# Forgetting attention in a two-block network: head sums moved later, scores negated, rounds written out, and the shared zone at a multiple of 128 bytes

## What is computed

```python
k = rmsnorm(k_s, k_norm)                      # per head, over 64 features
c = cumsum(log_sigmoid(f_logit))              # one number per head and token
q = rmsnorm(qg[..., :d], q_norm)
s = einsum('qd,kd->qk', q_i, k) * 64 ** -0.5 + c_i[..., None] - c[None, :]
s = where(kpos <= qpos, s, -inf)              # causal, blocks of 128 queries
p = softmax(s, axis=-1)
o = einsum('qk,kd->qd', p, v) * sigmoid(qg[..., d:])
x = x + o @ b_w_out
```

## Time and profile before

| | |
|---|---|
| median of three runs (lowest to highest) | 2271.34 us (2270.18 to 2273.8) |
| the profiled execution | 2267.01 us |
| its span, first to last instruction | 2265.3 us |
| share of the span busy: PE, POOL, DVE, ACT | 96%, 52%, 47%, 38% |
| mean granted TensorE clock | 0.989 of 2.4 GHz |
| the rounds, from the end of the first K unit to the output layer | about 1544 to 1855 us |

### The profile page before, as it was taken

How to read it: one execution, slowest core, us unless ns; L and a number is a source line. 1 busy time by engine, 2 the same in 40 slices (tenths; PEclk the granted TensorE clock), 3 DMA queues, 4 the chain that set the end, 5 groups by cost and what they waited for, 6 DMA issues and landing times.

```text
span 2265.3 us, 31096 instructions
## 1 busy us (share of the span) xinstructions
PE 2174.4 (96%) x9968; PEld 1744.3 (77%) x9968; DVE 1059.3 (47%) x1870; ACT 871.6 (38%) x1270; POOL 1175.9 (52%) x1572
## 2 busy tenths in 40 slices
PE   6999999799999999999999999998999989999999
PEld 5777666588888888888788888886677768888887
DVE  5466677533345543123435555115667664545400
ACT  6344223433344433232244443234444444443421
POOL 7443322777655555645456556654333325655653
PEclk9999999899999999999999999999999999999999
DMA  6213411233322233323223322332222202232332
GB/s 221 80 47 107 121 48 32 69 94 93 113 92 98 97 101 95 93 93 102 93 84 102 102 93 88 102 102 79 76 75 65 82 30 93 93 102 95 95 101 71
DMA packets 61469, 204.92 MB, mean 90 GB/s; under 512 B 6848, under 2 KB 6976, under 8 KB 61392
## 3 DMA queue, kind: packets, MB, share of 16 engines
q1 hardware_dynamic: 61200, 203.65, 28.1%
q10 hardware_dynamic: 192, 0.30, 0.1%
HBM read 201.52 MB, written 2.39 MB: 90 GB/s over the span
## 4 chain that ended last, share of the span: by engine, by line
PE 81%; DVE 8%; DVEq 4%; ACT 3%; issue 2%; POOL 1%; DMA 1%; ACTq 0%; SPq 0%
PE bank L1305 26%; PE bank L1307 26%; PE bank L1306 25%; PE bank L1513 1%; DVEq L1225 1%; DVE FX L1216 1%; PE bank L1567 1%; PE bank L1346 1%; DVE FX L1207 0%; DVE SS L1227 0%; DVEq L1231 0%; POOL YL L469 0%; DMA RAW<-in_w_att 0%; POOL WL L413 0%; ACT TD L729 0%
## 5 line engine op out<-in xcount | busy, mean ns | idle before, releaser
L413 POOL TENSOR_TENSOR WL<-RAW,WH 128x256 fp32r<-128x256 f32 x1496 | 1147.2, 800 | 1057.1 <-ACT WH L501 1056.9
L1305 PE MATMUL bank<-XH,WH 128*128 128x512 f32 x1840 | 730.2, 397 | 2.8 <-DVE XQ L821 2.0
L1307 PE MATMUL bank<-XH,WL 128*128 128x512 f32 x1840 | 716.7, 390 | 0.0
L1306 PE MATMUL bank<-XL,WH 128*128 128x512 f32 x1840 | 716.3, 389 | 0.0
L501 ACT ACTIVATE WH<-RAW 128x1024 fp32r<-128x1024 f32 x374 | 392.1, 1051 | 225.8 <-PE bank L1307 213.6
L1305 PEld LDWEIGHTS bank<-XH,WH 128*128 128x128 f32 x1840 | 345.4, 188 | 81.8 <-issue 6.6
L1306 PEld LDWEIGHTS bank<-XL,WH 128*128 128x128 f32 x1840 | 345.5, 188 | 76.3 <-issue 5.0
L1307 PEld LDWEIGHTS bank<-XH,WL 128*128 128x128 f32 x1840 | 345.4, 188 | 72.7
L1305 PE MATMUL bank<-FH,WH 128*128 128x512 f32 x528 | 208.0, 394 | 0.0
L1307 PE MATMUL bank<-FH,WL 128*128 128x512 f32 x528 | 207.0, 392 | 0.0
L1306 PE MATMUL bank<-FL,WH 128*128 128x512 f32 x528 | 204.9, 388 | 0.0
(11 more groups left out here) (276 smaller groups left out, 2342.1 us busy)
## 6 DMA issues: line engine op xcount, KB each, us to landing
RAW<-in_w_up SPq DMA_DIRECT2D x132, 512.0 KB, 3.5
RAW<-in_w_att SPq DMA_DIRECT2D x47, 512.0 KB, 3.6
RAW<-in_w_down SPq DMA_DIRECT2D x48, 448.0 KB, 3.3
RAW<-in_w_fa SPq DMA_DIRECT2D x32, 512.0 KB, 3.5
RAW<-in_w_down SPq DMA_DIRECT2D x24, 512.0 KB, 3.5
RAW<-in_w_ain SPq DMA_DIRECT2D x24, 512.0 KB, 3.5
RAW<-in_w_mrg SPq DMA_DIRECT2D x18, 512.0 KB, 3.6
RAW<-in_w_mrg SPq DMA_DIRECT2D x22, 256.0 KB, 2.7
```

The source lines that it names most:

```text
L413: last = nc.gpsimd.tensor_tensor(WL[:, s, w], RAW[:, s, w], WH[:, s, w].bitcast(F32), ALU.subtract)
L1305: mm(dst[:, 0:width], WH[:, s, w], a, start=start and k == 0, stop=False)
L1306: mm(dst[:, 0:width], WH[:, s, w], b, start=False, stop=False)
L1307: last = mm(dst[:, 0:width], WL[:, s, w], a, start=False, stop=stop and k == kc - 1)
```

## The change

1. **The zone** starts at the next multiple of 128 bytes. `HOLD` is gone; the fixed part ends at 135584 and the zone starts at 135680, which is 1060 times 128.
2. **Later head sums.** PE does the unit first and the head sum after it (K's sum after Q's unit, Q's after V's, V's transposes after the gate's unit). The raw head goes straight into `FK` or `FQ`. DVE uses it one group later than before, with four instructions for each head instead of six, and ACT reads the sum from PSUM itself.
3. **Negated scores.** The Q gain, the mask and the decay carry the opposite sign, the custom instruction finds a minimum, and that is the bias ACT needs: `HOLD` and the negation (L1211) go.
4. **The gate's** three ACT instructions move to the start of the next round, behind the exponentials of group 0.
5. **Rounds written out**, on all engines, instead of the loop.

```diff
-    zone = top[0]
+    zone = (top[0] + 127) // 128 * 128
...
-        with engine.Fori(0, (FA_PAIRS - 2) // 2) as i:
-            round_(2, i)
-            round_(3, i)
...
+        for p in range(FA_PAIRS + 1):
+            round_(p)
...
+        def squared(p, s):
+            act.wait_ge(q_raw, 2 * p + s + 1)
+            if 2 * p + s:
+                act.wait_ge(q_sum, 2 * p + s)
+            A_(SQ[:], (FK, FQ)[s][:, p % 2, :], ACT.Square).then_inc(q_sq, 1)
+        def head_rstd(p, s):
+            act.wait_ge(q_sum, 2 * p + s + 1)
+            if 2 * p + s:
+                act.wait_ge(f_epi, 2 * p + s)
+            A_(TD[:], LB[(O["fa"] + FA_L * p + 2 + 2 * s) % 2][:], ACT.Ln, scale=1.0 / 64, bias=EPSC[:, 0:1])
+            act.drain()
+            A_(TD[:], TD[:], ACT.Exp, scale=-0.5).then_inc(q_rs, 1)
...
+        def round_(p):
             for s in range(4):
                 if p < FA_PAIRS:
+                    hi(U["fa"], 4 * p + s + AHEAD, 0, 0)
+                if p < FA_PAIRS and s >= 2:
+                    head_rstd(p, s - 2)
                 if p >= 1:
...
+                        act.wait_ge(fs_read, 2 * g + j + 1)
+                        A_(FX[:, j, 0:nk], FX[:, j, 0:nk], ACT.Exp, scale=-1.0, bias=NX[:, j:j + 1],
                            accum_out=RS[:, j:j + 1]).then_inc(fp_exp, 1)
+                    if s == 0:
+                        out_gate(p - 1)
                 if p < FA_PAIRS and s < 2:
+                    squared(p, s)
...
+        def raw_head(p, s):
+            dve.wait_ge(unit_done, U["fa"] + 4 * p + s + 1)
+            v.tensor_tensor((FK, FQ)[s][:, p % 2, :], LB[(O["fa"] + FA_L * p + s) % 2][:], R[:], ALU.mult)\
+                .then_inc(lin_free, 1)
+            dve.drain().then_inc(q_raw, 1)
+        def head_sums(p, s):
+            dve.wait_ge(q_rs, 2 * p + s + 1)
+            v.scalar_tensor_tensor(out=SS[:], in0=LB[(O["fa"] + FA_L * p + 2 + 2 * s) % 2][:],
+                                   scalar=64 * EPS, in1=TD[:], op0=ALU.add, op1=ALU.mult).then_inc(lin_free, 1)
+            head = (FK, FQ)[s][:, p % 2, :]
+            v.scalar_tensor_tensor(out=head, in0=head, scalar=col(("kn", "qn")[s]), in1=TD[:],
+                                   op0=ALU.mult, op1=ALU.mult)
+            dve.drain()
+            v.scalar_tensor_tensor(out=SS[:], in0=SS[:], scalar=-0.5 / 64, in1=TD[:], op0=ALU.mult, op1=ALU.mult)
+            dve.drain()
+        def head_done(p, s):
+            head = (FK, FQ)[s][:, p % 2, :]
+            v.scalar_tensor_tensor(out=head, in0=SS[:], scalar=1.5, in1=head, op0=ALU.add, op1=ALU.mult)\
+                .then_inc(f_epi, 1)
...
-                        v.tensor_tensor(HOLD[:], EPSC[:, 0:1], EPSC[:, 1:2], ALU.add)
...
+                                               scale=1.0, scalar=-NEG, op0=ALU.add, op1=ALU.min,
+                                               accum_out=NX[:, j:j + 1]).then_inc(fs_read, 1)
+                if p < FA_PAIRS and s >= 2:
+                    head_sums(p, s - 2)
...
+                    f_unit(p, s, o0 + (0, 1, 3, 5)[s])
+                    if s == 1:
+                        f_sums(p, 0, o0 + 2)
+                    if s == 2:
+                        f_sums(p, 1, o0 + 4)
                     if s == 3:
+                        f_turn(p, o0 + 6)
```

More of the change, by code:

```diff
@@ L437, in _ @@
             pool.drain()
-            nc.gpsimd.affine_select(out=NM[r], in_=NM[r], compare_op=ALU.is_ge, fill=NEG, base=0,
+            nc.gpsimd.affine_select(out=NM[r], in_=NM[r], compare_op=ALU.is_ge, fill=-NEG, base=0,
                                     pattern=[[-64, 2], [1, P]], channel_multiplier=-1)
@@ L712, in o_split, with out_gate, round_ @@
             A_(AH[:, n, :], FY[:, n, :], ACT.Copy).then_inc(oh_ready, 1)
-        def round_(p, i=0):
+        def squared(p, s):
[10 more added lines that the diff above has]
+            A_(TD[:], TD[:], ACT.Exp, scale=-0.5).then_inc(q_rs, 1)
+        def out_gate(p):
+            g = FG[:, p % 2, :]
+            act.wait_ge(f_g, p + 1)
+            A_(g, g, ACT.Exp, scale=-1.0)
+            act.drain()
+            A_(g, g, ACT.Ln, bias=ONES[:, 0:1])
+            act.drain()
+            A_(g, g, ACT.Exp, scale=-1.0).then_inc(fg_ready, 1)
+        def round_(p):
             for s in range(4):
                 if p < FA_PAIRS:
-                    hi(U["fa"], 4 * p + s + AHEAD, i, 8)
+                    hi(U["fa"], 4 * p + s + AHEAD, 0, 0)
+                if p < FA_PAIRS and s >= 2:
+                    head_rstd(p, s - 2)
                 if p >= 1:
@@ L748, in round_ @@
                     act.dma_start(fc_d[:, :], FC[:, 1, :]).then_inc(fc_out, 16)
[L749 to L755, removed]
                 if p >= 1:
                     for j in range(2):
-                        act.wait_ge(ft_full, i * 16 + (2 * g + j + 1))
+                        act.wait_ge(ft_full, 2 * g + j + 1)
                         if g >= 1:
-                            act.wait_ge(fpv, i * 16 + (2 * g + j - 1))
+                            act.wait_ge(fpv, 2 * g + j - 1)
                         A_(FP[:, j, 0:nk], TRB[j][:, 0:nk], ACT.Copy).then_inc(ft_out, 1)
@@ L1218, in round_ @@
                 if p < FA_PAIRS:
[L1219 to L1245, removed]
                     if s >= 2:
-                        dve.wait_ge(unit_done, i * 8 + (U["fa"] + 4 * p + s + 1))
-                    b = LB[(o0 + (0, 2, 4, 6)[s]) % 2]
+                        head_done(p, s - 2)
                     if s < 2:
+                        raw_head(p, s)
                         if p == 0 and s == 0:
@@ L1515, in f_products, with f_unit, f_sums, f_turn @@
                 last.then_inc(fpv, 1)
-        def round_(p, i=0):
+        def f_unit(p, s, o):
+            pe.wait_ge(lin_free, o + 1)
+            xh, xl = ((XH, XL), (AH, AL), (XH, XL), (AH, AL))[s]
+            unit(U["fa"], 4 * p + s, 0, 0, KB, xh, xl, 0, LB[o % 2],
+                 ready=(al_ready, KB) if p == 0 and s == 1 else None)
+        def f_sums(p, s, o):
+            pe.wait_ge(lin_free, o + 1)
+            pe.wait_ge(q_sq, 2 * p + s + 1)
+            mm(LB[o % 2][:], BLK[:], SQ[:], start=True, stop=True).then_inc(q_sum, 1)
+        def f_turn(p, o):
+            pe.wait_ge(lin_free, o + 1)
+            pe.wait_ge(f_src, p + 1)
+            for k in range(TB):
+                last = nc.tensor.transpose(LB[o % 2][:, P * k:P * (k + 1)], TC[:, P * k:P * (k + 1)], IDN[:])
+            last.then_inc(f_trs, 1)
+        def round_(p):
             o0 = O["fa"] + FA_L * p
```

128 lines of the change are left out of this document (47 added, 81 removed).

## The result

The changed kernel takes 2259.18 us, median of five runs (2255.58 to 2261.66), against 2271.34, which is a median of five runs too, and not of three as the table of before has it; the ratio is 0.9948, 95% interval 0.9937 to 0.9960. It is faster by 0.5%, 12.2 us, where 27.8 were forecast; the time lies above the forecast range. The profiled execution took 2260.75 us with a span of 2259.0.

The account below looks back on a forecast made before the run. PE, busy 2174.4 of 2265.3 us, was taken as the bound, so gains come from its idle time, half clock or pace. 6.9 + 6.3 + 12.7 + 1.9 = 27.8 us off 2271.3 gives 2243.5 us; range 2236 to 2254.

Parts of the forecast that it names:

- Part 1: Matmul steps on zone tiles: starting the zone on a 128-byte line gains 6.9 us, bounds 0 and 7.5.
- the loop's 1 us: Rounds written out instead of looped: upper bound of the gain, 1 us, from branches; the forecast itself was 0.
- Part 2: Round 0, first K unit to first scores: Q's unit following at once shortens PE's stalls by 6.3 us, bounds 4.5 and 8.
- Part 3: Rounds 1 to 7: PE's waits before head sums and V's transposes vanish, 12.7 us, bounds 5 and 13.
- Part 4: Last round, without units: a shorter chain from scores to normalisation gains 1.9 us, bounds 0 and 4.
- Part 5: Rounds written out instead of the loop: gain 0, within 1 us either way.
- The zone's address means nothing: Rival on the zone's tiles: only the order counts, gain 20.9 us, time 2250.4 us; chance 0.16.
- Slack eaten: Rival for the seven rounds: a later ACT chain makes PE wait, 7 to 8 us lost, 2251 us; shared chance 0.16.
- slower: Rival: a much longer chain makes PE wait twice a round, slower than before, 2286 us with 3 us each; chance 0.04.
- Round 0 and the tail keep their stalls: Rival: first and last rounds keep their waits and half clock, 2251 us; shared chance 0.16.

Follow-up runs that it names:

- b_zone_up64: Kernel before the change with only the zone's start moved 64 bytes up, to the changed kernel's address; 2283.4 us, ratio 1.0058 to before.
- a_zone_64: Changed kernel with its zone 64 bytes lower, at the old address, leaving the new order; 2250.2 us, ratio 0.9911 to the kernel before.
- a_zone_plus128: Changed kernel with its zone 128 bytes further up, at 135808, the weights' remainder modulo 256; 2243.71 us, ratio 0.9882 to the kernel before.
- a64_chain_back: Changed kernel, zone at the old address, with tiny DVE instructions like HOLD and the negation put back around each custom instruction; 2251.66 us, ratio 0.9914 to before.

## Why the prediction was wrong, step by step

**Part 1 failed, and it accounts for the miss.** The step was "If a start off a 128-byte line costs the 7 ns". The rows had shown rightly that the pace with `FH` and `AH` differs from that with `XH` and that distance and stage do not explain it. What I took for the cause, a start off a 128-byte line, was one guess about a difference that has other properties: `XH` and the weights have the same remainder modulo 256, and the zone did not. Moving it from 64 to 128 bytes away made it worse. Measured in place of a gain of 6.9 us: a loss of 13 us (`b_zone_up64`), which 880 steps by 13.3 ns put at 11.7 (12.6 with `GH`'s 64). With this exchanged the forecast would have been 2243.5 + 6.9 + 11.7 = 2262; the time was 2259.2. The bound of this part was 0 on the bad side, and that closed the range too early. (The range's other end was added up wrongly: the upper bounds of parts 1, 2 and 4 and the loop's 1 us give 2243.5 - 0.6 - 1.7 - 2.1 - 1 = 2238.1, not 2236.) A step at 0.700, `GH`'s, stood in the earlier trace rows with the same start as `FH`: it said that a slower level exists, though the later profiles don't show it at that address. I read it as an extra gain to be had, not as the level to which the others could fall.

Of the Trainium skill, "TensorE: Matmul & The Clock Gate", part 1, gives one distance between warm matmuls, N/2.4 GHz plus about 2.5 ns. It names no address; that the distance holds wherever the operands lie was my reading. The runs differ, with 0.680 to 0.704 us for three matmuls by address alone, and the measurement decides. That the zone at a multiple of 128 would gain nothing, which I had worked out from that page and from the 16-byte cachelines that the Trainium skill gives in "SBUF — State Buffer", Specifications, was nearer to the result than my forecast.

**Part 2, round 0** was forecast at 6.3 us. From the norm to the first scores, before 1578.36 - 1537.9 = 40.5 us. The changed kernel on this stretch:

```profile
1559.95 0.51 PE L1308 MATMUL bank<-AH,WH 128*128 128x512 f32 x1 [1.97 <-DVE AL L1177]
...
1572.19 1.12 PE L1531 MATMUL bank<-SQ,BLK 128*128 128x512 f32 x2 [0.83 <-DVE SS L1204]
...
1575.81 0.79 PE L1308 MATMUL bank<-AH,WH 128*128 128x512 f32 x1 [2.50 <-DVE TC L1259]
...
1584.48 0.50 PE L1556 MATMUL bank<-FK,FQ 64*128 64x128 f32 x4
```

After it is 1584.48 - 1548.1 = 36.4, a gain of 4.1. In `a_zone_64` the scores start at 1570.91, 33.6 us after the norm, a gain of 6.9, and in `a_zone_plus128` 35.2 us after it, 5.3. The waits stand where they were worked out: the second half of `AL`, Q's sum behind the bank (0.83 us, forecast 1.1), the gate's unit behind the read of V (2.50, forecast 2.0). What varies is the half clock. Its stretches in this window sum to 10.2 us in the changed kernel (36.4 us) and in `a64_chain_back` (36.5), to 6.8 in `a_zone_plus128` (35.2) and to 3.4 in `a_zone_64` (33.6). The wait of 2.50 us is in all of them; in the changed kernel the clock falls to half at 1574.4, inside that wait, and stays there for 6.8 us. I had counted the half clock once and for another place. The gains of 4.1, 5.3 and 6.9 us lie around the 6.3 forecast and follow the half clock.

**Part 3, rounds 1 to 7**, 12.7 us: the mechanism and its size were right. The same three windows in the kernel before:

```profile
1537.90:1578.36 40.46, 29.62 (x108) 0.87 0.09 29
1578.36:1833.61 255.25, 242.57 (x1358) 1.00 0.24 80
1833.61:1906.10 72.49, 65.80 (x325) 0.93 0.18 59
```

From the first scores to those of the last round, 255.25 us became 243.36 in `a_zone_64`, 11.9 less. In the changed kernel the round fell by 1.7 us to 34.92, of which 16 steps with `AH` at 13 ns more take 0.2. No wait took the place of the old ones, but for 1.0 us for the normalised rows at the start of round 1 in `a_zone_64`, and `a64_chain_back` shows the slack. I was wrong on a side point: that `HOLD` and the negation gain nothing on PE is true of rounds 1 to 7 in the new order only.

**Part 4, the last round**, 1.9 us, was too small, within its bounds: 72.5 us became 69.4 in `a_zone_64`, 3.1 less, and 69.1 in `a_zone_plus128`, whose granted clock there is the 0.93 of before and of whose gain the 64 faster steps make 0.4. I had put `HOLD` at 0.15 us, where the earlier trace rows has a mean of 0.318. **Part 5**, 0, was right as far as can be measured. Parts 2 to 5 together: forecast 20.9, measured 20.3 by the median and 21.9 between the norms of `a_zone_64`, in the one of its four executions with a granted clock of 0.992 (the others had 0.988). No run moves the gate's three instructions (part 4 of the change) by themselves, so their share is not known.

**The rivals.** "The zone's address means nothing" had 0.16 and was wrong in the same direction: no case of mine had an address that costs. "Slack eaten" and "slower" are refuted by the waits. "Round 0 and the tail keep their stalls" is refuted too: both became shorter, by 6.9 and 3.1 us in `a_zone_64`.

## What to carry to other kernels

Where the rows show that one tile is faster than another, they don't show which of its properties makes it so. Before moving anything, list all that the fast one shares with its partners (here the remainder of the weights it is multiplied with), and give each reading its own sign and price. If matmuls run back to back, it is worth trying moving operands and weights at one remainder modulo 256: here it was worth 6.6 us alone, and 15 us against a round-looking address.

An instruction on DVE is free or not by the order around it: the same pairs cost PE 0.7 us a round where the next head waited behind them, and nothing in the steady rounds where the head was due one group later.

## What the runs showed of the hardware that I had not expected

- Three back-to-back matmuls of 512 columns take 0.680 us when the starts of the moving operands and of the weights agree modulo 256 bytes (up to 0.686 straight behind matmuls for which they don't). With both moving tiles 64, 128 and 192 bytes off they take 0.687, 0.697 and 0.700 with TensorE alone; in the whole kernel 64 bytes off gave 0.687 and 128 bytes off 0.700, and 192 was not run. Between two kernels that differ in nothing else, 64 bytes made 13 us of 2270.
- Starts that are no multiple of 64 behave irregularly (0.694 at +16, 0.680 at +240). Moving one operand of the four costs 6 to 24 ns in no order that I can state. No run shows the cause. Why `GH` had 0.700 in the one profile of before and 0.687 in four others at the same address stays open.
- Executions of one kernel differ by 1 to 7 us from the fastest to the slowest. The profiles of before and after had drifted 3.4 us apart within the first 640 us, where the change moves only addresses; the granted clock over them was 0.98 and 0.97, with half-clock stretches of 27.3 us in sum before and 37.5 after. That the stretches alone make the 3.4 us is not shown. A profile's difference in one stage therefore says more than the difference of two spans, and most where the stage's granted clock is the same in both.
